# A float32 encoder layer on one core: the weight stream's DRAM layout goes from [unit, partition, column] to [partition, unit, column]

## The reference, cut to what matters

```python
p = einsum('bsd,de->bse', x, w_in)              # q, k, v of both mixers, and both gates
h = layer_norm(ALPHA * x + (sigmoid(gA) * (yA @ w_proj_a) + sigmoid(gB) * (yB @ w_proj_b)) @ w_out)
q = (h @ w_query).reshape(n, 8, 2, 128)         # PEER: two half queries a head
v1, i1 = top_k(q[:, :, 0] @ sub_keys_1.T, 16)
v2, i2 = top_k(q[:, :, 1] @ sub_keys_2.T, 16)
sc, ci = top_k(v1[..., :, None] + v2[..., None, :], 16)
experts = e1 * 128 + e2                         # e1, e2 from i1, i2 by ci
u, v = take(u_table, experts), take(v_table, experts)   # tables of 16384 x 2048
w = softmax(sc) * gelu(einsum('nhkd,nd->nhk', u, h))
y = layer_norm(ALPHA * h + einsum('nhk,nhkd->nd', w, v))
```

## Time and profile before

| | us |
|---|---|
| median of 3 runs (lowest, highest) | 4710.53 (4706.78, 4716.7) |
| the profiled execution | 4703.39 |
| its span, first to last instruction | 4701.6 |
| TensorE busy (matmul) | 4333.9 |
| VectorE busy | 2686.9 |
| GpSimd busy | 2598.3 |
| ScalarE busy | 1065.4 |

### The profile page before, as it was taken

The page is one execution under the profiler, slowest core; times in us unless marked ns, Lnnn a source line. Parts: engine busy times, 40 slices in busy tenths (PEclk is TensorE's granted clock), DMA queues, the critical chain, the costliest instruction groups (busy, mean ns, idle before and its releaser), DMA issues.

```text
span 4701.6 us, 74886 instructions
## 1 busy us (share of the span) xinstructions
PE 4333.9 (92%) x26508; PEld 4161.2 (89%) x26508; DVE 2686.9 (57%) x4819; ACT 1065.4 (23%) x1872; POOL 2598.3 (55%) x1718
## 2 busy tenths in 40 slices
PE   8999999999989997986877888799999999999996
PEld 8999888888889996985776878799999999999995
DVE  1000233344432315997996777777777777777777
ACT  1000122222221102001221222223332333333223
POOL 4454322222235452442326766688787888888883
PEclk9999999999999999997998988899999999999998
DMA  5222322321243221211448998899999999999995
GB/s 200 96 96 103 113 105 105 125 74 72 82 142 122 95 95 47 69 56 61 171 157 325 381 366 344 329 391 385 390 393 377 385 393 390 390 384 394 392 391 219
DMA packets 265955, 1081.84 MB, mean 230 GB/s; under 512 B 24496, under 2 KB 89136, under 8 KB 181168
## 3 DMA queue, kind: packets, MB, share of 16 engines
q0 software_dynamic: 74736, 544.24, 28.4%
q1 hardware_dynamic: 87840, 388.01, 22.6%
q10 hardware_dynamic: 103328, 148.96, 9.3%
HBM read 1019.65 MB, written 66.85 MB: 231 GB/s over the span
## 4 chain that ended last, share of the span: by engine, by line
PE 49%; issue 21%; DVE 11%; POOL 11%; DMA 6%; ACT 1%; POOLq 0%; DVEq 0%; ACTq 0%
PE banks L464 29%; PE banks L642 6%; PE banks L706 5%; POOL w_lo L329 5%; POOL work L365 4%; DMA work<-in_u_rows,idx 3%; PE banks L533 2%; PE banks L495 1%; PE banks L694 1%; POOL rows_own L365 1%; PE banks L503 1%; DVE work L1390 1%; DVE work L1303 1%; DVE work L1311 1%; DVE mv_hi L1389 1%
## 5 line engine op out<-in xcount | busy, mean ns | idle before, releaser
L329 POOL TENSOR_TENSOR w_lo<-w_raw,w_hi 128x1024 fp32r<-128x1024 f32 x480 | 1159.4, 2416 | 421.5 <-ACT w_hi L1027 418.4
L335 POOL TENSOR_SCALAR w_hi<-w_raw 128x2048 fp32r<-128x2048 f32 x130 | 254.0, 1954 | 1480.2 <-PE banks L464 1268.8
L464 PE MATMUL banks<-mv_hi,w_hi 128*128 128x256 f32 x3648 | 863.9, 318 | 62.7 <-DVE mv_lo L1137 37.2
L464 PE MATMUL banks<-mv_lo,w_hi 128*128 128x256 f32 x3648 | 836.6, 311 | 0.0
L464 PE MATMUL banks<-mv_hi,w_lo 128*128 128x256 f32 x3648 | 835.3, 310 | 0.0
L706 PE MATMUL banks<-mv_hi,w_hi 128*128 128x384 f32 x2048 | 704.4, 344 | 103.8 <-DVE work L1442 79.5
L464 PEld LDWEIGHTS banks<-mv_hi,w_hi 128*128 128x128 f32 x3648 | 652.2, 189 | 127.2 <-issue 102.3
L1027 ACT ACTIVATE w_hi<-w_raw 128x1024 fp32r<-128x1024 f32 x480 | 507.1, 1059 | 1065.3 <-PE banks L706 779.4
L642 PE MATMUL banks<-mv_hi,w_hi 128*128 128x384 f32 x2048 | 701.3, 342 | 44.5 <-POOL w_lo L329 28.6
L706 PE MATMUL banks<-mv_lo,w_hi 128*128 128x384 f32 x2048 | 699.0, 341 | 0.0
L706 PE MATMUL banks<-mv_hi,w_lo 128*128 128x384 f32 x2048 | 697.9, 341 | 0.0
(11 more groups left out here) (159 smaller groups left out, 4821.3 us busy)
## 6 DMA issues: line engine op xcount, KB each, us to landing
w_raw<-in_wstream SPq DMA_DIRECT2D x480, 512.0 KB, 8.1
w_raw<-in_wstream SPq DMA_DIRECT2D x130, 1024.0 KB, 4.8
gate_matrix<-work ACTq DMA_DIRECT2D x12, 2048.0 KB, 6.3
work<-gate_matrix ACTq DMA_DIRECT2D x32, 768.0 KB, 13.1
out_p<-work ACTq DMA_DIRECT2D x34, 320.0 KB, 2.2
work<-out_p ACTq DMA_DIRECT2D x34, 320.0 KB, 3.5
gate_scratch<-work ACTq DMA_DIRECT2D x32, 320.0 KB, 2.2
work<-gate_scratch ACTq DMA_DIRECT2D x16, 640.0 KB, 3.9
```

The source lines that it names most:

```text
L329: pool.tensor_tensor(w_lo[s][:, part], raw[s][:, part], w_hi[s][:, part].bitcast(f32), ALU.subtract) \
L335: pool.tensor_scalar(w_hi[s][:, :], raw[s][:, :], 1.0, 0.0, ALU.mult, ALU.add).then_inc(hi_done, 1)
L464: last = pe.matmul(acc(dst, h), a[s][:, P * k:P * k + P], b[h][:, k, :], start=(k == k_first and n == 0), stop=(k == k_last and n == 2))
```

## The change

The host transposes the array: `wstream` becomes [partition, unit, column], of shape 128 x 370 x 2048. What one partition gets of all units is now contiguous, 370 x 8 KB = 2960 KB (185 x 16 KB). A whole unit is 128 pieces of 8 KB, each 2960 KB behind the last; a half is 128 pieces of 4 KB at the same distance. The DMAs in `_(sp)` name the same elements by the new axes. Their number, their order, their waits, their destination and the contiguous length of each row are the same. The lists of instructions of all five engines have the same rows before and after (PE 2780, DVE 1316, ACT 762, POOL 524, SP 25 rows, loops counted once).

```diff
             for s in range(2):
-                sp.dma_start(raw[s][:, :], wstream[s]).then_inc(raw_full[s], 16)
+                sp.dma_start(raw[s][:, :], wstream[:, s, :]).then_inc(raw_full[s], 16)
             with sp.Fori(1, U_LATE // 2) as i:
                 for s in range(2):
                     sp.wait_ge(split_done, 2 * i + s - 1)
-                    sp.dma_start(raw[s][:, :], wstream[ds(2 * i + s, 1)].rearrange("a p c -> p (a c)")) \
+                    sp.dma_start(raw[s][:, :], wstream[:, ds(2 * i + s, 1), :].rearrange("p a c -> p (a c)")) \
                         .then_inc(raw_full[s], 16)
...
-                    sp.dma_start(raw[s][:, half], wstream[U_LATE + s][:, half]).then_inc(raw_half[s][h], 16)
+                    sp.dma_start(raw[s][:, half], wstream[:, U_LATE + s, half]).then_inc(raw_half[s][h], 16)
...
-                        sp.dma_start(raw[s][:, half], wstream[ds(U_LATE + 2 * i + s, 1), :, half].rearrange("a p c -> p (a c)")) \
+                        sp.dma_start(raw[s][:, half], wstream[:, ds(U_LATE + 2 * i + s, 1), half].rearrange("p a c -> p (a c)")) \
                             .then_inc(raw_half[s][h], 16)
...
-    for name, arr in (("x_t", x_t), ("wstream", ws), ("u_rows", a["peer_u"]), ("v_rows", a["peer_v"]), ("cka", cka), ("cva", cva), ("ckb", ckb), ("cvb", cvb),
+    for name, arr in (("x_t", x_t), ("wstream", ws.transpose(1, 0, 2)), ("u_rows", a["peer_u"]), ("v_rows", a["peer_v"]), ("cka", cka), ("cva", cva), ("ckb", ckb), ("cvb", cvb),
```

## The result

The changed kernel takes 4676.53 us (median of 6 runs, 4666.25 to 4693.49), the kernel before 4713.09 us (6 runs, 4704.19 to 4717.64). The ratio is 0.993, with a 95% interval of 0.9916 to 0.9944: 0.7% faster, about 35 us. I had forecast no change, 4710 us, and a range down to 4688.

What follows compares the result with a forecast made beforehand. Stream far ahead to 2470 us; gathers chain the mixed trips; TensorE is the late groups' chain, DMA engines full too. Terms 0 + 0 + 0 left the median of 4710.53 us: forecast 4710 us, range 4688 to 4750.

Steps and rivals of the forecast that it cites:

- Instructions, packets, issue: All engines and SP's queue: same instructions, 87840 packets and 333 ns an issue, so 0.
- Whole units: The 130 whole-unit DMAs, to 2470 us: landing later by even 5 us would still be in time, so 0.
- the cover that was named: Whole units: TensorE's work on the unit before hides later landing; SP waited 18 us on average for each buffer.
- Half units in the late groups: Half-unit DMAs, TensorE and DMA engines both full: stream price unchanged at 43.0 us per MB, 0; gaps could save 14 us.
- Half units in the mixed trips: Half-unit DMAs beside gathers: price unchanged, 0; at the gathers' 39.1 us per MB, 18 us saved over 544 us.
- Fewer collisions: Rival, mixed trips: spreading close rows makes the stream cheaper; 20 us faster, 4690 us; chance 0.12.
- Its bound of 32 us: Largest saving, stream at 39.1 us per MB: 18 us in mixed trips, 14 us from TensorE's gaps in 3000 to 3600 us.
- its second sign: Sign of a cheaper stream: mixed trips shorter than 136 us each.
- Aliasing: Rival, half units from 2470 us: rows 2960 KB apart meet in one DRAM part; +36 us, 4746 us; chance 0.20.
- in_lnrow: One 8 KB row read by all 128 partitions, 41.5 us per MB; taken as partial bound on what regular distances cost.
- The rule of the Trainium skill: Rows a large power of two apart slow copies: 207 GB/s at 512 KiB, 164 at 2 MiB, 103 at 4 MiB; padding helps.
- My estimate from that page: If only the distance's size mattered: rate down about a fifth, 13 us per MB more, some 220 us on the whole.

Runs made afterwards that it cites:

- late_only: Kernel before with both layouts in DRAM and SP's last loop in two parts; only the late groups' units (178 to 369) read by partition: 0.9993.
- m_less: Kernel before, old layout; each half load of the mixed trips brings only the first 512 of its 1024 columns, 25 MB less read: 4681.07 us, 0.9953.
- half_block: Kernel before with the 240 half-loaded units stored as two 512 KB blocks each, one per half, so rows lie 4 KB apart: 0.9967.
- m_48: Kernel before with only the 48 units of the mixed trips stored by partition, without padding, rows 384 KB apart: 0.9933.
- m_64: Kernel before with only the 48 units of the mixed trips stored by partition, padded so that rows lie 512 KB apart: 0.9934.

## Why the prediction was wrong, point by point

**Instructions, packets, issue: 0.** Right: the packets are the same, and so are SP's 333 ns an issue.

**Whole units: 0.** Right, and by the cover that was named. The stream even became dearer there: from 43.9 to 46.2 us per MB (15.7% and 92.50 MB in 300 to 2000 us). That is more than chance: the 15 traces whose whole units have the old layout lie between 43.9 and 44.6. Neither the landing of 4.8 us nor the gate loads' start at 2468 us shows more than 3 us of it. "When it runs alone" was a wrong reading: ScalarE's queue moved 70.53 MB beside the stream in this stretch; only the gathers were absent.

**Half units in the late groups: 0.** Right: `late_only` 0.9993. The price went from 43.0 to 42.5 us per MB (33.5% and 37.84 MB in 3600 to 3900 us), and the gaps of TensorE from which the bound took 14 us stayed: from the last gate load shown to the end of the groups it was busy 1533 of 1543 us before and 1532 of 1542 after.

**Half units in the mixed trips: 0, and at most -18 us.** This is the step that failed. I priced the stream by the engine time of its packets and bounded the gain by that price falling to the gathers' 39.1 us per MB. The price did not move (44.3 to 44.1), and the trips with the group behind them lost 39 us. The sum had no term for the landing: how long a DMA waits for the last of its 16 increments once the first has come. That spread fell from 1.8 to 1.2 us for the gathers, which is most of the fall of their mean landing from 9.3 to 8.5 us, and VectorE waits for gathers in this stage. The share of 0.94 in the earlier trace rows stood beside the late groups' 1.00 and was the hint. I take it as imbalance, DMA engines that stand idle while another still works on the same DMA, and not as spare room; the first half of that is argued, the second is what `m_less` bears out.

**The rivals.** "Fewer collisions" had the sign and the place (mixed trips), and somewhat over half of the size: 20 us of gain against 36.6. It had 0.12. Its mechanism, packets that get cheaper, did not come: no price near 39 to 41. Its bound of 32 us was near the gain by luck, as 14 of them were the late groups', which gave nothing, and 18 the mixed trips', where 39.3 us arose (the group behind them included). Nor could its second sign tell much, since three of the four trips before were already shorter than 136 us from load to load (112.7, 131.9 and 134.5). Aliasing did not come at 2960 KB; at 2 and 4 MB a loss of its kind did.

**The sources weighed.** `in_lnrow`, where all engines read one row, bounded nothing: at 4 MB the price is 76.9 against its 41.5. One row read by all is no stand-in for 128 rows that alias. The gathers' lower price was put down to the packet length, 4 KB against 8, and scattered rows were called free on that ground; but the earlier trace rows have 8 KB packets at 43.9, no cheaper than the 4 KB ones at 43.0, so the difference has no cause shown. The rule of the Trainium skill ("DMA: Bandwidth & Descriptors", section "Latency and other measured facts") was borne out: slow at 2 MiB (50.1 us per MB), slower at 4 MiB (76.9), full at 512 KiB (43.8), and helped by padding. The page measured copies from DRAM to DRAM, and has the full rate back with 4 KiB; here 8 KB of padding at 4 MB took the ratio from 1.0455 to 0.9978 and 64 KB to 0.9946, still short of 0.9933. The other remedy that it names, to "lay tiles out contiguously", is safe here too, but contiguous units in the mixed trips cost the kernel 0.65% against rows 384 KB to 2960 KB apart. My estimate from that page was also off in its sum: a rate lower by a fifth makes 43.0 / 0.8 = 53.8 us per MB, 11 more and not 13, and some 180 us and not 220.

**What stays open.** Shown: the distance between a DMA's rows makes the gain, in the mixed trips alone, where TensorE waits by way of VectorE for DMAs, and with an unchanged price; and gathers' landings get shorter at their end. Argued only: that it is the slowest DMA engine. The spread goes roughly along with the ratio in the table but not in `half_block` and `m_less`, the ratio is from many runs and the spread from one trace, and the trace does not say which engine an increment came from. Which parts of DRAM the rows meet in was not measured.

No version beat the changed kernel: `m_48` (0.9933) and `m_64` (0.9934) equal it (0.993).

## What to carry to other kernels

Bound a change of DRAM layout by landing times and by the DMA engines' idle share in the stage that waits for any DMA, not by the price of the packets that are moved: transfers that nobody waits for slow the ones beside them. Where a ring of few buffers waits for landings, try rows some 384 KB or more apart, and keep every distance between rows off 2 MB and 4 MB: with all units at 4 MB the kernel took 19% longer. The price of one row that all partitions read (41.5 us per MB) told nothing of how regular distances behave (76.9 at 4 MB).

## What the runs showed of the hardware that I had not expected

A contiguous megabyte is not the fastest source when other queues are busy: with rows of the stream 384 KB apart gathers landed after 8.7 us in place of 9.3, with rows 2960 KB apart after 8.5, at nearly the same engine time per MB. Without gathers beside it, in 300 to 2000 us, the contiguous unit was the cheaper one (43.9 against 46.2 us per MB). And half rows of 4 KB exactly 2 MB or 4 MB apart cost 50.1 and 76.9 us per MB, while 2960 KB apart they cost 44.1.
